# Feed-forward of a hybrid two-block network: first-half weight remainders of the second block's up slabs move from VectorE to GpSimd, and VectorE steps are reordered in attention and at stage borders

## The chip, the cores and the metric

One core of one Trainium2 chip. The metric is the device time of one execution in microseconds (us), smaller is better. Everything is float32 data of 256 tokens by 1024 channels, kept in SBUF from beginning to end, while the weights stream in from HBM.

## The reference

Two blocks of two layers each. The first block: a convolution mixer (layer 0), a recurrence with dilated attention (layer 1), each followed by a feed-forward `(silu(conv(h @ w_gate)) * (h @ w_up)) @ w_down` of width 2816. The second block (layers 2 and 3 here): `x = x + hybrid_mixer(rms_norm(x))`, then

```python
def conv_glu_ffn_2(h, w_up, conv_w, conv_b, w_down):
    u = causal_dwconv_2(h @ w_up, conv_w, conv_b)      # 3 taps, both halves
    gate, val = u[..., :FFN_DIM], u[..., FFN_DIM:]
    return (jax.nn.silu(gate) * val) @ w_down
```

## The kernel before, in words

**Slabs.** All weights are cut into slabs of 128 x 2 x 1024 float32 (two halves of 512 KB). The slabs of all stages form one numbered stream. Each half of a slab passes through four hands: SyncE loads it into `w_raw` (L604), ScalarE rounds it to a high part `w_hi` (L1520, `weights_hi`), VectorE or GpSimd subtracts to get the remainder `w_lo` (`split_lo`, L565), and TensorE multiplies. There are three slots (`WSLOTS = 3`); ScalarE works three slabs ahead (`ROUND_AHEAD`), the remainders two (`SPLIT_AHEAD`). A remainder of half 0 or 1 increments `w_lo[0]` or `w_lo[1]`, always in the order of the slabs; where another engine continues that count, it waits for the one before it (`take_over`, L571). The same count frees `w_raw` for the load of the slab three further on.

**Operands** are also split in two, a rounded and a rest part; `lo_part` (L574) makes a rest.

**The feed-forward** has 22 up slabs, `upA` (14) and `upB` (8), and 12 down slabs, `dnA` (4, between `upA` and `upB`) and `dnB` (8). Layers 2 and 3 are `NORMED_UP`: from up slab 2 on, TensorE works by `paired_halves` (L812 on): eight products of 512 columns with the high part of half 0 (L817), one of half 1, then `slab.wait_split(pe, 0)`, the eight remainder products of 256 columns of half 0 (L821), then `wait_split(pe, 1)`, those of half 1, and the last seven high products.

**Around each up slab c.** ScalarE (`up`, L1590 on) waits until TensorE is done with c, copies two sums out of PSUM (L1595) and increments `up_rest`, rounds a half of slab c + 3, makes the first tap of c (L1604), rounds the hidden value of c - 1 (L1585), rounds the other half, and computes silu (L1617). VectorE (`up`, L2174 on) waits for `up_rest`, adds the two sums (L2182), makes the half 0 remainder of slab c + 2, then the older taps (L2164), the half 1 remainder, and the product of gate and value (L2215), which increments `ffn_prod`. VectorE does this for all up slabs of all four layers, but in layers 2 and 3 the remainders of up slabs 2 and 3 (both halves) are GpSimd's (L697 to 704). GpSimd's loop `up` (L705 on), for slab n, is otherwise only the rest part of the hidden value:

```python
hi, lo = ffn_parts(layer, n)
if n + 2 < count:
    pool.wait_ge(s.up_rest, UP_BEFORE[layer] + off + n + 3 - UP_FIRST[layer])
pool.wait_ge(s.hid_hi, base + off + n + 1)
lo_part(pool, lo, prod[:, j % 2:j % 2 + 1, :], hi).then_inc(s.hid_split, 1)
```

`up_rest` stands at `UP_BEFORE + c + 1 - UP_FIRST` once ScalarE has copied slab c, so this line waits for slab n + 2.

**Elsewhere.** In the dilated attention of layer 1 VectorE masks (`at_mask`, L2373), ScalarE takes exp (`at_exp`), VectorE normalises (`at_probs`), TensorE transposes; the eight units share two `score` buffers. `residual` of ScalarE and GpSimd and `add_residual` of VectorE (L2121) close a stage: the sum into x, the squares for the next norm (`fold_squares`), the rest parts of the next operand (`norm_lo`). In the mixers of layers 2 and 3, `by_token` transposes and the `gates` slabs' remainders of half 1 (VectorE) lie among the state-space steps.

Of the kernel before, what the change touches and what calls it, by code (L numbers as in the profile page):

```python
# [14 lines left out]
P = 128  # L15
# [180 lines left out]
def build(nc, dram):  # L196
    ctx = ExitStack()
    with ctx:  # L198
# [213 lines left out]
        eps = sb("eps", [P, 1])  # L412
        acc = sb("acc", [P, 2, 2, T])
        sil = std[:, :, T:2 * T]
        score = arena[:, 57 * T:65 * T].rearrange("p (b n) -> p b n", b=2)
        cum_parts = sb("cum_parts", [P, T], BF16)
        cum_mid = sb("cum_mid", [SH, T], BF16)
        ident_b = sb("ident_b", [P, SH], BF16)
# [215 lines left out]
        def _(pool):  # L634
# [55 lines left out]
            def ffn(f, n, l=None):  # L690

                sfx, base = stage_ffn(f, l)
                layer = n // 2 - 1

                if layer in NORMED_UP:
                    take_over(pool, "upA" + sfx, 1, l)
                    for k in range(2):  # L697
                        for half in range(2):
                            if k == 1 and half == 1:
                                pool.wait_ge(s.ffn2_tap, 4 * l * FC + 4)  # L700
                            split_lo(pool, slab_at("upA" + sfx, k, l).ahead(SPLIT_AHEAD), half)
                        if k == 0:
                            scaled_lo(UP_OPENING[layer], raw_set(layer))

                def up(off, count):  # L705
                    def body(slab, n, j):
                        hi, lo = ffn_parts(layer, n)
                        if n + 2 < count:
                            pool.wait_ge(s.up_rest, UP_BEFORE[layer] + off + n + 3 - UP_FIRST[layer])
                        pool.wait_ge(s.hid_hi, base + off + n + 1)  # L710
                        lo_part(pool, lo, prod[:, j % 2:j % 2 + 1, :], hi).then_inc(s.hid_split, 1)
                    return body
                slabs("upA" + sfx, up(0, UP_A), l)
                slabs("upB" + sfx, up(UP_A, FC - UP_A), l)
                take_over(pool, "dnB" + sfx, 0, l)
                residual("dnB" + sfx, n, l)

            nc.gpsimd.memset(zeros, 0.0)
# [8 lines left out]

            norm_lo(0, range(DC // 2))
            add_squares(0, 1)
            add_squares(0, 2)  # L730
            pool.wait_ge(s.w_lo[0], 1)
            split_lo(pool, Slab(s, 1), 0)
            opening("ev_cf", 0)
            for stage in ("ev_sc", "ev_b"):
# [58 lines left out]
        def _(pe):  # L793
# [429 lines left out]
            def at_transposes(u):  # L1223
                t = u % 2
                pe.wait_ge(s.at_p, u + 1)
                if u == 0:
                    pe.wait_ge(s.qk_std, COUNT["od_qk"])
                else:
                    pe.wait_ge(s.at_pt, u)
                for b in range(DIL_G * (t + 1)):  # L1230
                    where = tr[:, b * P:b * P + P] if b < 4 else stat[:, T + (b - 4) * P:T + (b - 3) * P]
                    mm = nc.tensor.transpose(where, score[:, u % 2, b * P:b * P + P], ident)
                mm.then_inc(s.at_tr, 1)

            def at_values(p):
# [54 lines left out]
            def layer(l):  # L1290
# [86 lines left out]
                for u in range(4):  # L1377
                    t, kv = u // 2, u % 2
                    if u < 3:
                        pe.wait_ge(s.da_masked, 4 * l + u + 1)  # L1380
                        da_logits(u + 1)
                    pe.wait_ge(s.da_p, 4 * l + u + 1)
                    if u == 0:
                        pe.wait_ge(s.dt_tok, l + 1)
                    else:
                        pe.wait_ge(s.da_out, 4 * l + u)
                    for st in range(t + 1):
                        if st == 1:
                            pe.wait_ge(s.xt_copied, 8 * l + 2 * u)
                        for i in range(QPK):  # L1390
                            mm = nc.tensor.transpose((tr, stat)[st][:, i * P:i * P + P],
                                                     da_score[u % 2][:, i, st * P:st * P + P], ident)
                    mm.then_inc(s.da_tr, 1)
                    slab_products(slab_at("z", 2 * u, l), operand)
                    pe.wait_ge(s.da_pt, 6 * l + (1, 2, 4, 6)[u])
                    for st in range(t + 1):
                        mm = nc.tensor.matmul(tr[:, :], v2[:, st, kv * P:kv * P + P], pt[:, st, 0:4 * P],
                                              start=(st == 0), stop=(st == t))
                    mm.then_inc(s.da_pv, 1)
                    by_token(2 * u)  # L1400
                    if u == 3:
                        pe.wait_ge(s.a_exp, l + 1)
                        pe.wait_ge(s.cum_lo, l + 1)
                        running_sums(0)
                        running_sums(1)
                    if u == 1:
                        slab_products(slab_at("z", 2 * u + 1, l), operand, between=lambda: by_token(3))
                    else:
                        slab_products(slab_at("z", 2 * u + 1, l), operand)
                        by_token(2 * u + 1)  # L1410
# [100 lines left out]
        def _(act):  # L1511
# [36 lines left out]
            def residual(stage, n, gain=None, l=None):  # L1548
# [3 lines left out]
                for k in range(COUNT[stage]):  # L1552
# [12 lines left out]
                            square(j)  # L1565
                    if j == 2 and gain is None:
                        done(slab)
                    if j == 2:
                        root_table()
                if gain is None:  # L1570
                    norm_root(n)
# [241 lines left out]
            def at_exp(u):  # L1813
                n = DIL_G * (u % 2 + 1) * P
                act.wait_ge(s.at_masked, u + 1)
                nc.scalar.activation(score[:, u % 2, 0:n], score[:, u % 2, 0:n], ACT.Exp, scale=-1.0,
                                     bias=small[:, 16 + u:17 + u], accum_out=small[:, 24 + u:25 + u]).then_inc(s.at_exp, 1)

            def at_copy(u):
# [217 lines left out]
        def _(dve):  # L2037
# [80 lines left out]
            def add_residual(stage, l=None, n=None):  # L2118
# [5 lines left out]
                def body(slab, k, j):  # L2124
                    if k < COUNT[stage] - late:
                        weights(slab, halves)
                    if n is not None and k > COUNT[stage] - 4:
                        fold_squares(n, j - 1)
                    slab.wait_done(dve)

# [14 lines left out]
                    if n is not None and j >= 2 and k >= COUNT[stage] - 2:  # L2145
                        if j == 2:
                            weights(slab)
                        norm_lo(n, (2 * j, 2 * j + 1))
                        if j == 3:
                            fold_squares(n, 3)  # L2150
                            weights(slab)
                slabs(stage, body, l)
# [17 lines left out]
            def ffn(f, n, l=None, beside_dn=None):  # L2170
# [3 lines left out]
                def up(off):  # L2174
                    def body(slab, n, j):
# [14 lines left out]
                            tt(zz[:, j, :, :], lin[slab.bank][:, :, :], std[:, 0, 0:T].unsqueeze(1).to_broadcast([P, 2, T]),  # L2190
                               ALU.mult).then_inc(s.bank_free[slab.bank], 1)
                        if c == 2 and layer in NORMED_UP:
                            for half in range(2):
                                dve.wait_ge(s.w_lo[half], slab.number + SPLIT_AHEAD)
                        if opened or layer not in NORMED_UP:
                            weights(slab, (0,))
                        if l is None:
                            dve.wait_ge(s.ffn_t0, base + c + 1)
# [25 lines left out]
                slabs("upA" + sfx, up(0), l)  # L2224
                if beside_dn is not None:
                    beside_dn[0]()
                add_residual("dnA" + sfx, l)
                if beside_dn is not None:
                    beside_dn[1]()
# [144 lines left out]
            def at_mask(u):  # L2374
# [1 line left out]
                t = u % 2  # L2376
                n = (t + 1) * P
                dve.wait_ge(s.at_logits, u + 1)
                if u >= 2:
                    dve.wait_ge(s.at_tr, u - 1)  # L2380
                sc3 = score[:, u % 2, 0:DIL_G * n].rearrange("p (g k) -> p g k", g=DIL_G)
                nc.vector.tensor_tensor_reduce(
                    sc3, at_logit(t),
                    dil[:, DIL_AT[t]:DIL_AT[t] + DIL_G * n].rearrange("p (g k) -> p g k", g=DIL_G),
# [4 lines left out]
            def at_probs(u):  # L2389
                n = (u % 2 + 1) * P  # L2390
                dve.wait_ge(s.at_exp, u + 1)
                ac.link(nc.vector.reciprocal(small[:, 32 + u:33 + u], small[:, 24 + u:25 + u]))
                ts(score[:, u % 2, 0:DIL_G * n], score[:, u % 2, 0:DIL_G * n], small[:, 32 + u:33 + u], None, ALU.mult)\
                    .then_inc(s.at_p, 1)

            qk_norm(0)
# [19 lines left out]
            at_mask(1)  # L2416
            at_probs(0)
            tt(lru_hs[:, :, :], lru_hs[:, :, :], lru_gate[:, :, :], ALU.mult).then_inc(s.lru_y, 1)
            at_mask(2)
            at_probs(1)  # L2420
            dve.wait_ge(s.lru_y_hi, 1)
            lo_part(nc.vector, raw_set(1)[1][:, 0:NC4, :], lru_hs[:, :, :], raw_set(1)[0][:, 0:NC4, :]).then_inc(s.lru_y_lo, 1)
            at_mask(3)
            for u in range(2, 2 * DIL_H):
                if u < 2 * DIL_H - 2:
                    at_probs(u)
                if u == 2 * DIL_H - 3:
                    at_probs(u + 1)
                if u + 2 < 2 * DIL_H:
                    at_mask(u + 2)  # L2430
            at_probs(2 * DIL_H - 1)
            dve.wait_ge(s.att_hi, 1)
            lo_part(nc.vector, raw_set(1)[1][:, NC4:NC4 + 2, :], acc[:, 0, :, :], raw_set(1)[0][:, NC4:NC4 + 2, :]).then_inc(s.att_lo, 1)
            take_over(dve, "od_out", 1)
# [4 lines left out]
            def layer(l):  # L2439
# [236 lines left out]
                def ssd_pair(m):  # L2676
                    if m % 2 == 0:
                        ssd_group(m // 2)
                    ssd_m(2 * m, 2 * m)
                    ssd_m(2 * m + 1, 2 * m + 1)  # L2680
                ssd_pair(0)
                for m in range(XCH // 2):
                    if m + 1 < XCH // 2:
                        ssd_seg(2 * m + 2)
                        ssd_seg(2 * m + 3)
                    if m != 3:
                        weights(slab_at("gates", m, l))
                    ssd_out(2 * m, 2 * m)
                    ssd_out(2 * m + 1, 2 * m + 1)
                    if m == 3:  # L2690
                        weights(slab_at("gates", m, l))
                    if m + 1 < XCH // 2:
                        ssd_pair(m + 1)
# [287 lines left out]
```

## Time and profile before

| | us |
|---|---|
| median of 3 runs (lowest to highest) | 1682.47 (1680.27 to 1682.65) |
| the profiled execution's own time | 1679.26 |
| its span, first to last instruction | 1677.5 |
| TensorE busy | 1654.3 |
| VectorE busy | 1333.7 |
| ScalarE busy | 1086.0 |
| GpSimd busy | 752.4 |

The span is what the trace covers; the 1.8 us between it and the execution's own time lie around it. A share of busy time near 100% says that hardly any time is to be had from that engine's waits, not that it couldn't be made to wait.

### The profile page before, as it was taken

The page shows a single profiled execution, that of the slowest core. Times are in us where ns is not written, and L with a number is a line of the kernel's source. Part 1 is how long each engine was busy: PE and PEld are TensorE (multiplying, and loading weights), DVE is VectorE, ACT ScalarE, POOL GpSimd, SP SyncE. Part 2 cuts the span into 40 slices and gives each one's busy share as a digit, 9 for nine tenths or more (in the row PEclk, how much of TensorE's full clock was granted, in tenths as well). Part 3 has the DMA queues.
Part 4 walks back from the last instruction along what each step waited for, and adds up shares of the span by engine and source line. Part 5 has one row for each costly group of instructions (what it writes and reads, how often), then busy time and mean ns, then how long its engine had stood idle before and what let it go on. Part 6 is the DMA issues. An engine that isn't in the chain of part 4 may idle for free. (4 is left out here: it accounts for less than half of the span.)

```text
span 1677.5 us, 28519 instructions
## 1 busy us (share of the span) xinstructions
PE 1654.3 (99%) x10944; PEld 1491.6 (89%) x10944; DVE 1333.7 (80%) x2204; ACT 1086.0 (65%) x1828; POOL 752.4 (45%) x448
## 2 busy tenths in 40 slices
PE   9999999999999999999999999999999999999997
PEld 8998889998888899998788988899999878888887
DVE  7968887495887887885896699778886689579795
ACT  7676665676765584767653776657577665378572
POOL 7631105872110367764654521057675465351113
PEclk9999999999999999999999999999999999999999
DMA  8445646542555655453445456555455335546552
GB/s 300 163 156 188 223 156 198 189 126 86 179 190 188 195 177 189 165 175 120 137 160 190 153 175 213 166 186 198 153 172 171 126 126 176 176 145 202 191 181 86
DMA packets 81240, 287.10 MB, mean 171 GB/s; under 512 B 9169, under 2 KB 9681, under 8 KB 80977
## 3 DMA queue, kind: packets, MB, share of 16 engines
q1 hardware_dynamic: 79776, 282.10, 50.7%
q10 hardware_dynamic: 1328, 3.18, 0.5%
q8 instruction: 87, 1.43, 0.3%
q14 instruction: 49, 0.39, 0.1%
HBM read 283.90 MB, written 1.05 MB: 170 GB/s over the span
## 5 line engine op out<-in xcount | busy, mean ns | idle before, releaser
L565 POOL TENSOR_TENSOR w_lo<-w_raw,w_hi 128x1024 fp32r<-128x1024 f32 (+2 forms) x239 | 568.4, 2398 | 364.1 <-ACT w_hi L1520 283.0
L1520 ACT ACTIVATE w_hi<-w_raw 128x1024 fp32r<-128x1024 f32 (+1 forms) x544 | 543.1, 1033 | 253.6 <-PE lin L798 163.0
L565 DVE TENSOR_TENSOR w_lo<-w_raw,w_hi 128x1024 fp32r<-128x1024 f32 (+1 forms) x305 | 444.7, 1462 | 30.7 <-ACT w_hi L1520 29.7
L796 PE MATMUL lin<-hid_pair,w_hi 128*128 128x256 f32 x1152 | 329.9, 286 | 1.7 <-DVE hid_pair L574 1.7
L797 PE MATMUL lin<-hid_pair,w_hi 128*128 128x256 f32 x1152 | 325.9, 283 | 0.0
L798 PE MATMUL lin<-hid_pair,w_lo 128*128 128x256 f32 x1152 | 325.9, 283 | 0.0
L796 PEld LDWEIGHTS lin<-hid_pair,w_hi 128*128 128x128 f32 x1152 | 220.9, 192 | 4.1 <-issue 3.3
L797 PEld LDWEIGHTS lin<-hid_pair,w_hi 128*128 128x128 f32 x1152 | 221.0, 192 | 0.3
L798 PEld LDWEIGHTS lin<-hid_pair,w_lo 128*128 128x128 f32 x1152 | 220.9, 192 | 0.0
L574 POOL TENSOR_TENSOR hid_pair<-arena,hid_pair 128x256 fp32r<-128x256 f32 x64 | 56.5, 887 | 294.4 <-ACT std L1595 175.7
L817 PE MATMUL logit<-h_pair,w_hi 128*128 128x512 f32 x540 | 146.7, 392 | 0.0
L817 PE MATMUL lin<-h_pair,w_hi 128*128 128x512 f32 x540 | 135.0, 390 | 3.2 <-DVE arena L2182 2.8
L2164 DVE SCALAR_TENSOR_TENSOR acc<-arena,par,acc 128x254 f32<-128x254 f32 (+1 forms) x264 | 119.8, 495 | 7.5 <-ACT acc L1604 4.6
L817 PEld LDWEIGHTS lin<-h_pair,w_hi 128*128 128x128 f32 x540 | 101.1, 188 | 25.4 <-DVE arena L2182 3.7
L817 PEld LDWEIGHTS logit<-h_pair,w_hi 128*128 128x128 f32 x540 | 97.2, 189 | 17.4
L796 PE MATMUL lin<-h_pair,w_hi 128*128 128x256 f32 x320 | 92.9, 290 | 0.9 <-DVE h_pair L574 0.8
L797 PE MATMUL lin<-h_pair,w_hi 128*128 128x256 f32 x320 | 90.5, 283 | 0.0
L798 PE MATMUL lin<-h_pair,w_lo 128*128 128x256 f32 x320 | 90.5, 283 | 0.0
L817 PE MATMUL logit<-hid_pair,w_hi 128*128 128x512 f32 x324 | 89.1, 392 | 0.0
L796 PE MATMUL lin<-w_hi,hid_pair 128*128 128x512 f32 (+1 forms) x224 | 87.0, 388 | 0.0
L797 PE MATMUL lin<-w_lo,hid_pair 128*128 128x512 f32 (+1 forms) x224 | 84.0, 375 | 0.0
L798 PE MATMUL lin<-w_hi,hid_pair 128*128 128x512 f32 (+1 forms) x224 | 84.0, 375 | 0.0
(413 smaller groups left out, 3508.2 us busy)
## 6 DMA issues: line engine op xcount, KB each, us to landing
w_raw<-in_upA SPq DMA_DIRECT2D x112, 512.0 KB, 4.4
w_raw<-in_upB SPq DMA_DIRECT2D x64, 512.0 KB, 4.6
w_raw<-in_xbc SPq DMA_DIRECT2D x48, 512.0 KB, 4.3
w_raw<-in_dnA SPq DMA_DIRECT2D x32, 512.0 KB, 4.3
w_raw<-in_dnB SPq DMA_DIRECT2D x32, 512.0 KB, 3.9
w_raw<-in_z SPq DMA_DIRECT2D x32, 512.0 KB, 4.5
w_raw<-in_gates SPq DMA_DIRECT2D x32, 512.0 KB, 4.1
w_raw<-in_ps SPq DMA_DIRECT2D x32, 512.0 KB, 4.0
```

The costliest lines, as they stand in the source:

```text
L565: eng.tensor_tensor(w_lo[slab.slot][:, half, part], w_raw[slab.slot][:, half, part], w_hi[slab.slot][:, half, part].bitcast(F32), ALU.subt ...
L574: return eng.tensor_tensor(lo, whole, hi.bitcast(F32), ALU.subtract)
L796: nc.tensor.matmul(out, lhs[0], rhs[0], start=first, stop=False)
L797: nc.tensor.matmul(out, lhs[0], rhs[1], start=False, stop=False)
L798: return nc.tensor.matmul(out, lhs[1], rhs[0], start=False, stop=last)
L817: return nc.tensor.matmul(outs[half], tile_of(slab, half, k)[0], pairs[k], start=(k == 0), stop=(half == 1 and k == last))
L1520: nc.scalar.activation(w_hi[slab.slot][:, half, part], w_raw[slab.slot][:, half, part], ACT.Copy)\
L2164: ins = stt(outs[i][:, d:T], ins_[i][:, 0:T - d], weight(taps - 1 - d, i), outs[i][:, d:T], ALU.mult, ALU.add)
```

## The change

In the up stages of layers 2 and 3, GpSimd makes the half 0 remainder of slab n + 2 at the head of its body for slab n, from n = 2 of `upA` to the end of `upB`; VectorE makes it no more there, and takes the count over at `dnA`, GpSimd at `upB`. GpSimd's remainder of half 1 of up slab 3 waits for the first product of VectorE, not for its first taps. In the attention there are three `score` buffers, and VectorE's masks and normalisations come in another order. At a stage border `fold_squares(n, 2)` comes behind the last residual sum instead of ahead of it; for `od_out`, `norm_lo` of chunks 4 and 5 and the loading of ScalarE's root table also come later. One `by_token` moves between two halves of a `z` slab, one `gates` remainder behind two other steps, and at the start two lines of GpSimd change places.

```diff
-        score = arena[:, 57 * T:65 * T].rearrange("p (b n) -> p b n", b=2)
+        score = arena[:, 57 * T:66 * T].rearrange("p (b n) -> p b n", b=3)
@@ GpSimd, ffn
                             if k == 1 and half == 1:
-                                pool.wait_ge(s.ffn2_tap, 4 * l * FC + 4)
+                                pool.wait_ge(s.ffn_prod, base + 1)
                             split_lo(pool, slab_at("upA" + sfx, k, l).ahead(SPLIT_AHEAD), half)
@@
                         hi, lo = ffn_parts(layer, n)
+                        if layer in NORMED_UP and off + n >= 2:
+                            split_lo(pool, slab.ahead(SPLIT_AHEAD), 0)
                         if n + 2 < count:
                             pool.wait_ge(s.up_rest, UP_BEFORE[layer] + off + n + 3 - UP_FIRST[layer])
                         pool.wait_ge(s.hid_hi, base + off + n + 1)
@@
                 slabs("upA" + sfx, up(0, UP_A), l)
+                if layer in NORMED_UP:
+                    take_over(pool, "upB" + sfx, 0, l)
                 slabs("upB" + sfx, up(UP_A, FC - UP_A), l)
-                take_over(pool, "dnB" + sfx, 0, l)
+                if layer not in NORMED_UP:
+                    take_over(pool, "dnB" + sfx, 0, l)
@@ GpSimd, start
+            pool.wait_ge(s.w_lo[0], 1)
             add_squares(0, 2)
-            pool.wait_ge(s.w_lo[0], 1)
@@ TensorE, z slabs
-                    if u == 1:
-                        slab_products(slab_at("z", 2 * u + 1, l), operand, between=lambda: by_token(3))
+                    if u in (1, 2):
+                        slab_products(slab_at("z", 2 * u + 1, l), operand, between=lambda: by_token(2 * u + 1))
@@ ScalarE, residual
-                    if j == 2:
+                    if j == (3 if stage == "od_out" else 2):
                         root_table()
@@ VectorE, add_residual
-                    if n is not None and k > COUNT[stage] - 4:
+                    if n is not None and COUNT[stage] - 4 < k < COUNT[stage] - 1:
                         fold_squares(n, j - 1)
                     slab.wait_done(dve)
@@
                         if j == 2:
                             weights(slab)
-                        norm_lo(n, (2 * j, 2 * j + 1))
+                            if stage != "od_out":
+                                norm_lo(n, (4, 5))
                         if j == 3:
+                            if stage == "od_out":
+                                norm_lo(n, (4, 5))
+                            fold_squares(n, 2)
+                            norm_lo(n, (6, 7))
                             fold_squares(n, 3)
@@ VectorE, ffn
                         if c == 2 and layer in NORMED_UP:
-                            for half in range(2):
-                                dve.wait_ge(s.w_lo[half], slab.number + SPLIT_AHEAD)
-                        if opened or layer not in NORMED_UP:
+                            dve.wait_ge(s.w_lo[1], slab.number + SPLIT_AHEAD)
+                        if layer not in NORMED_UP:
                             weights(slab, (0,))
@@
+                if layer in NORMED_UP:
+                    take_over(dve, "dnA" + sfx, 0, l)
                 add_residual("dnA" + sfx, l)
@@ VectorE, attention
-                if u >= 2:
-                    dve.wait_ge(s.at_tr, u - 1)
-                sc3 = score[:, u % 2, 0:DIL_G * n].rearrange("p (g k) -> p g k", g=DIL_G)
+                if u >= 3:
+                    dve.wait_ge(s.at_tr, u - 2)
+                sc3 = score[:, u % 3, 0:DIL_G * n].rearrange("p (g k) -> p g k", g=DIL_G)
@@
-            at_mask(2)
             at_probs(1)
             dve.wait_ge(s.lru_y_hi, 1)
             lo_part(nc.vector, raw_set(1)[1][:, 0:NC4, :], lru_hs[:, :, :], raw_set(1)[0][:, 0:NC4, :]).then_inc(s.lru_y_lo, 1)
+            at_mask(2)
             at_mask(3)
             for u in range(2, 2 * DIL_H):
-                if u < 2 * DIL_H - 2:
-                    at_probs(u)
-                if u == 2 * DIL_H - 3:
-                    at_probs(u + 1)
+                at_probs(u)
                 if u + 2 < 2 * DIL_H:
                     at_mask(u + 2)
-            at_probs(2 * DIL_H - 1)
@@ VectorE, gates
-                    if m != 3:
+                    if m not in LATE_WEIGHTS:          # (3, 5)
                         weights(slab_at("gates", m, l))
                     ssd_out(2 * m, 2 * m)
                     ssd_out(2 * m + 1, 2 * m + 1)
-                    if m == 3:
+                    if m in LATE_WEIGHTS:
                         weights(slab_at("gates", m, l))
```

## Rows read from the trace of the kernel before

**Rows 1.** The page: busy us of the engines (share, instructions); granted TensorE clock, 40 slices.

```profile
PE 1654.3 (99%) x10944; PEld 1491.6 (89%) x10944; DVE 1333.7 (80%) x2204; ACT 1086.0 (65%) x1828; POOL 752.4 (45%) x448
...
PEclk9999999999999999999999999999999999999999
```

**Rows 2.** Waits of TensorE (who waited for whom: us in total, times, longest).

```profile
PE lin L817 <- DVE arena L2182: 2.8, 2, 1.4
...
PE lin L796 <- DVE hid_pair L574: 1.7, 1, 1.7
PE logit L821 <- DVE w_lo L565: 1.3, 2, 0.7
...
PE tr L1421 <- DVE sq L2668: 0.8, 2, 0.4
...
PE lin L796 <- DVE h_pair L574: 0.8, 1, 0.8
PE stat L1391 <- DVE arena L2617: 0.7, 2, 0.3
```

**Rows 3.** Timeline, all engines, one up slab of layer 2 (start, us, what, [idle before]).

```profile
1006.02 1.98 PE L817 MATMUL lin<-h_pair,w_hi 128*128 128x512 f32 x8
1006.22 0.38 ACT L1595 ACTIVATE std<-lin 128x256 f32<-128x256 f32 x1 [1.23 <-PE logit L817]
...
1006.76 1.06 ACT L1520 ACTIVATE w_hi<-w_raw 128x1024 fp32r<-128x1024 f32 x1
1006.91 0.42 DVE L2182 TENSOR_TENSOR arena<-lin,std 128x256 f32<-128x256 f32 x1 [0.51 <-ACT std L1595]
1006.95 0.74 POOL L574 TENSOR_TENSOR hid_pair<-arena,hid_pair 128x256 fp32r<-128x256 f32 x1 [4.83 <-ACT std L1595]
...
1007.58 1.22 DVE L565 TENSOR_TENSOR w_lo<-w_raw,w_hi 128x1024 fp32r<-128x1024 f32 x1
...
1007.83 1.13 PEld L821 LDWEIGHTS lin<-h_pair,w_lo 128*128 128x128 f32 x8
...
1008.83 1.67 DVE L2164 SCALAR_TENSOR_TENSOR acc<-arena,par,acc 128x255 f32<-128x255 f32 x4
...
1010.41 1.22 DVE L565 TENSOR_TENSOR w_lo<-w_raw,w_hi 128x1024 fp32r<-128x1024 f32 x1
...
1011.58 1.98 PE L817 MATMUL lin<-h_pair,w_hi 128*128 128x512 f32 x8
```

**Rows 4.** Waits over all engines: GpSimd's hidden-rest subtraction behind ScalarE's copy, layers 2, 3.

```profile
POOL hid_pair L574 <- ACT std L1595: 175.7, 28, 30.6
...
POOL hid_far L574 <- ACT std L1595: 38.6, 8, 4.8
```

**Rows 5.** Groups by form, GpSimd: weight remainder (busy, mean ns, idle before and releasers).

```profile
L565 POOL TENSOR_TENSOR w_lo<-w_raw,w_hi 128x1024 fp32r<-128x1024 f32 x213 | 519.4, 2459 | 293.9 <-ACT w_hi L1520 220.2 <-PE logit L1374 32.3 <-DVE w_lo L565 13.2
```

**Rows 6.** Timeline, opening of the up stage of layer 2 (the same 532 us later in layer 3).

```profile
964.00 2.39 POOL L565 TENSOR_TENSOR w_lo<-w_raw,w_hi 128x1024 fp32r<-128x1024 f32 x1 [2.56 <-DVE acc L2164]
964.01 2.66 DVE L2215 TENSOR_TENSOR arena<-std,acc 128x256 f32<-128x256 f32 x1
964.42 1.98 PE L817 MATMUL lin<-h_pair,w_hi 128*128 128x512 f32 x8
...
971.54 2.14 PE L817 MATMUL lin<-h_pair,w_hi 128*128 128x512 f32 x8 [1.40 <-DVE arena L2182]
...
974.29 0.37 ACT L1595 ACTIVATE std<-lin 128x256 f32<-128x256 f32 x1
...
978.18 1.98 PE L817 MATMUL lin<-h_pair,w_hi 128*128 128x512 f32 x8
```

**Rows 7.** Timeline, attention of layer 1: VectorE's remainder behind GpSimd's.

```profile
380.72 1.82 POOL L565 TENSOR_TENSOR w_lo<-w_raw,w_hi 128x768 fp32r<-128x768 f32 x1 [4.12 <-ACT w_hi L1520]
380.76 2.85 DVE L574 TENSOR_TENSOR hid_pair<-arena,hid_pair 128x1024 fp32r<-128x1024 f32 x1
```

**Rows 8.** DMA of layer 2's feed-forward: halves of up slabs (count, KB, median us to landing).

```profile
w_raw<-in_upA SPq DMA_DIRECT2D x16, 512.0 KB, 4.5
```

More of the change, by code:

```diff
@@ L1231, in at_transposes @@
                     where = tr[:, b * P:b * P + P] if b < 4 else stat[:, T + (b - 4) * P:T + (b - 3) * P]
-                    mm = nc.tensor.transpose(where, score[:, u % 2, b * P:b * P + P], ident)
+                    mm = nc.tensor.transpose(where, score[:, u % 3, b * P:b * P + P], ident)
                 mm.then_inc(s.at_tr, 1)
@@ L1815, in at_exp @@
                 act.wait_ge(s.at_masked, u + 1)
-                nc.scalar.activation(score[:, u % 2, 0:n], score[:, u % 2, 0:n], ACT.Exp, scale=-1.0,
+                nc.scalar.activation(score[:, u % 3, 0:n], score[:, u % 3, 0:n], ACT.Exp, scale=-1.0,
                                      bias=small[:, 16 + u:17 + u], accum_out=small[:, 24 + u:25 + u]).then_inc(s.at_exp, 1)
@@ L2392, in at_probs @@
                 ac.link(nc.vector.reciprocal(small[:, 32 + u:33 + u], small[:, 24 + u:25 + u]))
-                ts(score[:, u % 2, 0:DIL_G * n], score[:, u % 2, 0:DIL_G * n], small[:, 32 + u:33 + u], None, ALU.mult)\
+                ts(score[:, u % 3, 0:DIL_G * n], score[:, u % 3, 0:DIL_G * n], small[:, 32 + u:33 + u], None, ALU.mult)\
                     .then_inc(s.at_p, 1)
@@ L2680, in ssd_pair @@
                     ssd_m(2 * m + 1, 2 * m + 1)
+                LATE_WEIGHTS = (3, 5)
                 ssd_pair(0)
```

## The prediction

> **What bounds the kernel now.** The page comes first: TensorE is busy for 1654.3 of 1677.5 us, at the upper clock level (2.4 GHz) in all 40 slices [rows 1]. So at most 23 us could be won from its waits, and 80% of VectorE or 45% of GpSimd says nothing by itself: work moved between them pays only where TensorE waits for it, and costs wherever it comes to wait. The second view is the waits of TensorE [rows 2]. Those that touch the change are small: 2.8 us in two waits for VectorE's sum in the up stages of layers 2 and 3, 1.3 us in two for a weight remainder there, 1.7 and 0.8 us in layer 1, 0.7 and 0.8 us in the mixers. The third view is the timeline of one up slab in layer 2 [rows 3], to be read as a list of deadlines. TensorE starts it at 1006.02 and the next at 1011.58, a period of 5.57 us. It needs the half 0 remainder at 1007.83 (the weight load of L821), 1.81 us after the start. VectorE has it ready long before, as it makes it two slabs ahead. VectorE's own list (two sums of 0.42, two remainders of 1.22, four taps of 1.67, a product of 0.42) is 5.4 of the 5.57 us: full, but in time, since from one slab to the next TensorE starts without a wait.
>
> **The main part: half 0 on GpSimd.** What counts is not GpSimd's load but its order. In its body for slab n the new remainder (for slab n + 2) stands first, and behind it the old wait for `up_rest` of slab n + 2. That wait really is the last to end there: GpSimd's rest of the hidden value starts right behind ScalarE's copy 28 + 8 = 36 times [rows 4], which is 12 + 6 in each of two layers, all bodies with n + 2 < count. Queued behind the wait is now the head of the next body: the remainder for slab n + 3. But `up_rest` of n + 2 comes when TensorE is done with n + 2, that is, when it has started n + 3, whose remainder has not been begun. Two slabs of lead become none.
>
> The price per slab, from TensorE's start of the slab at 1006.02 [rows 3]: ScalarE copies twice from 1006.22, GpSimd's rest subtraction starts at 1006.95 and lasts 0.74, so it is free at 1007.69, 1.67 after the start. A remainder of 1024 columns takes 2459 ns in the mean on GpSimd [rows 5], mostly about 2.40 (2.39 in [rows 6]). I take 2.40, since in the stretch concerned VectorE has nothing to run until its taps: ready at 4.07, and with 0.1 us for the two semaphore steps at 4.17. It is needed at 1.81, so TensorE waits 2.36 us, in every such slab, as each slab's copy comes from TensorE's own end: a loop that cannot catch up. Nothing covers it; TensorE has no other work between L817 and L821.
>
> The count: in `upA` the remainder stands behind a wait in bodies 2 to 12 (slabs 4 to 13 and `dnA` 0: 11), in `upB` in bodies 1 to 6 (slabs 3 to 7 and `dnB` 0: 6). Body 0 of `upB` has no wait ahead of it; body 13 of `upA` and body 7 of `upB` wait only for `hid_hi`, and their targets are a whole slab later. That is 17 per layer, of which slab 4 is apart.
>
> The opening [rows 6]. Before, GpSimd's half 1 of slab 3 starts at 964.00, at the same time as VectorE's first product, which then takes 2.66 us in place of 0.42 and ends with it. The changed wait makes the product go first, so VectorE gains 2.2 us and GpSimd loses 0.45. The half is then ready at about 966.9, and TensorE needs it about 2.8 us after its start of slab 3 at 964.42, so at 967.2: just in time. ScalarE's copies for slab 2 come about 1.4 earlier, VectorE's sum with them, and the wait of 1.40 ahead of slab 4 (971.54) goes: it can start at 964.42 + 5.57 = 970.0. But its remainder hangs on the copies for slab 3, which ScalarE, behind TensorE here, makes at 974.29 and would make at some 973.1 to 973.7. Plus 0.66 + 0.74 + 2.40 + 0.1 the remainder is there at 976.9; needed at 971.8 to 972.0. Slab 4 ends at about 970.0 + 5.57 + 4.9 = 980.5, where before slab 5 starts at 978.18: 2.3 us later, with the gained 1.4 and the old remainder wait of 0.66 [rows 2] already in it.
>
> Sum per layer: 2.3 + 16 x 2.36 = 40.1 us; two layers 80 us. What VectorE saves (17 times 1.22 and more) is worth nothing beyond the opening, since it was not waited for. Its taps may be blocked until GpSimd is done: from 4.07 they, the half 1 remainder and the product take 1.67 + 1.22 + 0.42, till 7.4, within the new period of 7.93. The load of half 0 is issued when the remainder is done, 4.1 after the start; landing takes 4.5 us [rows 8], so 8.6, and ScalarE wants it at 7.93 + 0.74 = 8.67 [rows 3]. Tight, but ScalarE's copies stand ahead of it. The take-over at `dnA` holds VectorE until about 7.2 us after the start of `dnA` 0; its next sums are due behind that slab anyway: nothing.
>
> In [rows 6] a VectorE operation with both inputs in SBUF ends only with the GpSimd one it met. The Trainium skill, page "SBUF — State Buffer", section "Who interferes with whom", calls this an exclusive lock of a shared port pair held for the whole instruction; by that rule alone the move would exchange 1.22 us of VectorE for up to 2.40 us of blocking, a loss where VectorE has 0.2 us to spare, while by the rows the stall of TensorE comes first and gives VectorE its time back.
>
> **The other parts.** Attention: TensorE waits 1.69 us for VectorE's rest part, which takes 2.85 us in place of about 1.2, beside GpSimd's remainder at 380.72 [rows 2, 7]. Ahead of it stood a mask that itself waited for logits; with that mask behind it, it starts at about 379.1 and is done before 380.72: -1.7. The plain order of the later units could move some tenths either way; I take 0. Border of `od_out`: the residual sum comes earlier, two rest parts later, the wait of 0.8 us [rows 2] falls to about 0.3: -0.5. At the other borders TensorE did not wait and its next operand parts are not put off: 0. The `z` transposes (two waits, 0.7) and the `gates` remainder at m = 5 (two waits, 0.8): both go at best, -1.5; at worst none does. At the start, the first remainder is done ahead of the last squares, so the exchanged wait is met already: 0. Together -3.7 us, bounds 0 and -6.
>
> **Sum** against the profiled execution: 1679.26 + 80.2 - 3.7 = 1755.8 us. It ran 3.2 us below the median; on the median the same difference of 76.5 gives 1759.0.
>
> **Bounds of the main term.** Least: with the mean lead of the copies 0.1 shorter, no semaphore time, the remainder at 2.39: 2.2 per slab, 75 in all. A GpSimd operation that yields to a started VectorE operation could add 0.4 per slab: 2.76, 94 in all. With the bounds of the rest: +69 to +94.
>
> **Rivals.**
> First, no lateness (faster). If the count in `up_rest` meant a slab earlier, the remainder would be ready one period before: 4.07 - 5.57 = 1.5 us ahead of the start, with 3.3 to spare. It decides at GpSimd's chain of 4.17 us against the 1.81 of TensorE. Then only the small waits are won: 2.8 + 1.3 + 3.7 = 7.8, so 1674.7. Against it stand the 36 releases by ScalarE's copy of the slab that has just ended [rows 3, 4]. Chance 0.04.
> Second, the loop gets longer through ScalarE: the late load (8.6 against 8.67) and blocked taps push silu past the end of the slab, and the copies with it. At 0.5 to 1 us in each of 34 slabs, +17 to +34: 1776 to 1793. For it speaks that both margins are under 0.6 us; against, that the copies come ahead of the rounding that needs the load. Chance 0.07.
> Third, TensorE's clock. Every slice was granted 2.4 GHz [rows 1], with waits of at most 1.7 us past the start [rows 2]; the new ones are 2.4 and 4.9 us. If it fell to 1.2 GHz in these 34 slabs, each would take 11.1 us, and the remainder would be nearly in time, so +3.2 us a slab over the forecast: +108, 1867. The Trainium skill, page "TensorE: Matmul & The Clock Gate", section "What's actually happening", lets the clock fall after idleness; by that the two waits of 4.9 us are the likeliest place. If only there, it costs a few us, inside the range. Chance of the full case 0.03.
> The forecast keeps 0.86.
>
> **Range and chances.** The main case spans 1751 to 1776; for its unseen ends (a shorter chain, a brief clock fall, some of the second rival) I take 1746 to 1778. About 0.2% (3.4 us) is what a measurement of this kernel tells from no change. Slower 0.95, same 0.01, faster 0.04.
>
> **What would show it.** Right: in the changed trace TensorE waits over 2 us at L821 for GpSimd's L565 in 34 places, a period of about 7.9 us in the up stages, a first such wait of about 5 us; the wait at 971.54 and the long product at 964.01 gone; total waits of TensorE up by about 77 us; the wait of 1.7 us in attention gone. Wrong: GpSimd's remainder starting before ScalarE's copies of the slab ahead, a period of 5.57 kept, or a granted clock below 1.

## The result, and the profile after

The changed kernel takes 1771.93 us (median of 4 runs, 1770.28 to 1772.96) against 1682.22 before: ratio 1.0535, 95% interval 1.0516 to 1.0553. It is 89.7 us slower; 76.5 were forecast, and the time lies inside the range. The profiled execution has a span of 1768.5 us, 91.0 more than before.

The page of the changed kernel, its first and second part:

```profile
span 1768.5 us, 28515 instructions
PE 1685.1 (95%) x10944; PEld 1508.9 (85%) x10944; DVE 1312.5 (74%) x2164; ACT 1084.3 (61%) x1828; POOL 845.9 (48%) x488
...
PE   9999999999999999999998779899999999977978
...
PEclk9999999999999999999999889999999999989999
```

40 remainders have moved (DVE x2204 to x2164, POOL x448 to x488). TensorE's busy time has grown by 30.8 us though it does the same 10944 products: part of them ran at the lower clock, in the slices where its busy share is down too. These are the up stages of layers 2 and 3.

The waits of TensorE (who waited for whom: us in total, times, longest), the longest four:

```profile
PE lin L826 <- POOL w_lo L565: 68.8, 34, 4.9
PE logit L1087 <- POOL arena L731: 2.1, 1, 2.1
PE lin L1104 <- DVE h_pair L574: 1.0, 1, 1.0
PE stat L1132 <- ACT arena L1739: 0.7, 1, 0.7
```

L826 is L821 of the kernel before. 34 waits for GpSimd's weight remainder, one of 4.9 us in each layer, the others of 1.85. Of [rows 2] the 2.8, the 1.3 and the 1.7 are gone.

One up slab of layer 2 in the timeline (start, us, what, idle before); it answers to [rows 3]:

```profile
1003.09 1.98 PE L822 MATMUL lin<-h_pair,w_hi 128*128 128x512 f32 x8
1003.29 0.38 ACT L1600 ACTIVATE std<-lin 128x256 f32<-128x256 f32 x1 [3.89 <-PE logit L822]
...
1004.02 0.75 POOL L574 TENSOR_TENSOR hid_pair<-arena,hid_pair 128x256 fp32r<-128x256 f32 x1 [6.14 <-ACT std L1600]
...
1004.73 2.36 POOL L565 TENSOR_TENSOR w_lo<-w_raw,w_hi 128x1024 fp32r<-128x1024 f32 x1
...
1005.90 2.65 DVE L2174 SCALAR_TENSOR_TENSOR acc<-arena,par,acc 128x255 f32<-128x255 f32 x4 [1.16 <-ACT acc L1609]
...
1007.14 1.00 PEld L826 LDWEIGHTS lin<-h_pair,w_lo 128*128 128x128 f32 x8 [2.27 <-POOL w_lo L565]
...
1010.76 1.98 PE L822 MATMUL lin<-h_pair,w_hi 128*128 128x512 f32 x8
```

The loop is there as described: TensorE's end, ScalarE's copies, GpSimd's rest part, GpSimd's remainder, TensorE again. The load of the remainder comes 4.05 us after the start of the slab (1007.14 - 1003.09), where before it came at 1.81, and the period is 7.67 us in place of 5.57: 2.10 more. VectorE's taps take 2.65 us in place of 1.67, as they hardly advance until GpSimd's remainder ends (1004.73 + 2.36 = 1007.09).

Not every slab is that short. The differences between the starts of the slabs in layer 2, read from the timeline of TensorE, are these periods from up slab 2 on (each of them 5.57 before, except 6.02, 7.12 and 6.64 for slabs 2, 3 and 4); `dnA` 1 to `upB` 2, which don't wait, are left out:

```
slab   2     3     4      5    6     7     8     9     10    11    12    13    dnA0
us     5.84  5.59  12.32  9.20 7.67  9.21  7.67  9.23  7.67  9.22  7.67  7.67  9.20
upB    3     4     5     6     7     dnB0
us     7.67  7.67  9.20  7.67  9.21  7.67
```

Layer 3 has seven long ones too (and 12.59 for slab 4): 14 slabs of 9.2. What they are is seen in the stretches (us, busy and instructions of the engines, PEclk, DMA share, GB/s) of one of them and of a short one:

```profile
996.00:1000.00 4.00, 2.15 (x15) 2.07 (x15) 3.31 (x5) 2.33 (x5) 1.88 (x1) 0.88 0.27 65
1000.00:1004.00 4.00, 4.00 (x16) 3.33 (x16) 0.84 (x3) 0.71 (x3) 0.00 (x0) 0.69 0.53 202
...
1008.00:1012.00 4.00, 4.00 (x24) 3.51 (x24) 2.37 (x6) 1.46 (x4) 0.30 (x1) 1.00 0.80 262
```

After the wait that ends at 997.93 the granted clock is below full until about 1003 (16 products in 4 us); after the one that ends at 1007.14 it is 1.00 (24 products in 4 us). Between 1000 and 1004 it was at its lower level, 1.2 GHz, for part of the time.

The 91 us between the two profiled spans, by stages (the clock's part in slab 4 is in its row):

| | us |
|---|---|
| 32 slabs, 2.10 each | +67.2 |
| 14 of them, 1.54 each for the clock | +21.6 |
| slab 4, two layers (12.32, 12.59 against 6.64) | +11.6 |
| slabs 2 and 3, two layers (5.84 + 5.59 against 6.02 + 7.12) | -3.4 |
| start -1.2, attention and the border of `od_out` -2.9, mixers of layers 2 and 3 -1.0 each | -6.1 |

### The profile page after: what moved, and what is told of

Same layout as the page of the kernel before. It is cut to its first block and busy times, and to the rows that moved or that the text cites. A ratio compares the mean times of both kernels' runs of the same rounds, so it can differ in the third digit from the quotient of the medians.

```text
span 1768.5 us, 28515 instructions
## 1 busy us (share of the span) xinstructions
PE 1685.1 (95%) x10944; PEld 1508.9 (85%) x10944; DVE 1312.5 (74%) x2164; ACT 1084.3 (61%) x1828; POOL 845.9 (48%) x488
## 5 line engine op out<-in xcount | busy, mean ns | idle before, releaser
L565 POOL TENSOR_TENSOR w_lo<-w_raw,w_hi 128x1024 fp32r<-128x1024 f32 (+1 forms) x279 | 664.9, 2397 | 385.8 <-ACT w_hi L1525 306.4
L565 DVE TENSOR_TENSOR w_lo<-w_raw,w_hi 128x1024 fp32r<-128x1024 f32 (+1 forms) x265 | 392.8, 1487 | 37.9 <-ACT w_hi L1525 36.9
L2174 DVE SCALAR_TENSOR_TENSOR acc<-arena,par,acc 128x254 f32<-128x254 f32 (+1 forms) x264 | 162.4, 654 | 52.9 <-ACT acc L1609 51.4
L822 PE MATMUL logit<-h_pair,w_hi 128*128 128x512 f32 x540 | 157.6, 416 | 0.0
L826 PE MATMUL lin<-h_pair,w_lo 128*128 128x256 f32 x540 | 81.1, 293 | 61.5 <-POOL w_lo L565 61.5
L826 PEld LDWEIGHTS lin<-h_pair,w_lo 128*128 128x128 f32 x540 | 73.1, 194 | 77.0 <-POOL w_lo L565 74.1
L822 PEld LDWEIGHTS logit<-h_pair,w_hi 128*128 128x128 f32 x540 | 106.5, 207 | 20.0
L803 PE MATMUL lin<-h_pair,w_lo 128*128 128x256 f32 x320 | 90.5, 283 | 0.0
L801 PE MATMUL lin<-w_hi,hid_pair 128*128 128x512 f32 (+1 forms) x224 | 87.0, 388 | 0.0
```

What stands on the lines that cost most here:

```text
L565: eng.tensor_tensor(w_lo[slab.slot][:, half, part], w_raw[slab.slot][:, half, part], w_hi[slab.slot][:, half, part].bitcast(F32), ALU.subt ...
L801: nc.tensor.matmul(out, lhs[0], rhs[0], start=first, stop=False)
L803: return nc.tensor.matmul(out, lhs[1], rhs[0], start=False, stop=last)
L822: return nc.tensor.matmul(outs[half], tile_of(slab, half, k)[0], pairs[k], start=(k == 0), stop=(half == 1 and k == last))
L826: return nc.tensor.matmul(outs[half][:, 0, :], tile_of(slab, half, k)[1], pairs[k][:, 0, :], start=False, stop=(half == 0 and k == last))
L2174: ins = stt(outs[i][:, d:T], ins_[i][:, 0:T - d], weight(taps - 1 - d, i), outs[i][:, d:T], ALU.mult, ALU.add)
```

## The experiments

**Half 0 back on VectorE.** All else stays as changed.

```diff
-                        if layer in NORMED_UP and off + n >= 2:
-                            split_lo(pool, slab.ahead(SPLIT_AHEAD), 0)
...
-                        if layer not in NORMED_UP:
+                        if opened or layer not in NORMED_UP:
                             weights(slab, (0,))
```

(with the hand-overs at `upB`, `dnA` and `dnB` as before)

> The changed kernel with one part undone: VectorE makes the half 0 remainders of the up slabs of layers 2 and 3 again, everything else stays as changed. Theory (the remainder queued behind the wait for the slab just ended is the whole loss): the 34 waits of 4.9 and 1.85 us are gone, the period of an up slab is 5.57 us again, TensorE's clock is 1.00 throughout, and the small gains stay: about 1674 us, 8 below the kernel before. Rival (some of the loss comes from the reordered borders, attention or gates): it stays above 1682.

1669.33 us, ratio 0.9941 to the kernel before (0.9926 to 0.9956), granted clock 0.999. The period is 5.57 us again and no wait for GpSimd's remainder is left in the up stages. So the move of half 0 costs 102.6 us (1771.93 - 1669.33), and all the rest of the change gains, by more than forecast. This version is faster than both kernels, by 0.6% than the one before.

**Without the wait for `up_rest`.** GpSimd keeps half 0.

```diff
-                        if n + 2 < count:
+                        if n + 2 < count and layer not in NORMED_UP:
                             pool.wait_ge(s.up_rest, ...)
```

> The changed kernel, GpSimd's half 0 remainders kept, but its rest subtraction no longer waits for up_rest of slab n + 2 in layers 2 and 3 (only for the rounded hidden value of n, which ScalarE makes one slab earlier). Order theory: the remainder for slab n + 3 is ready some 6.5 us after the start of slab n + 2, a slab ahead of its use, so TensorE does not wait for it: within 1674 to 1682. Rival (GpSimd's remainder of 2.4 us in place of VectorE's 1.2 us, and the blocking between the two engines, is what costs): VectorE's taps are blocked behind it, its work for a slab grows to over 5.57 us, and 0.3 to 0.6 us a slab are lost, 1685 to 1700.

1748.68 us, ratio 1.0413 (1.0396 to 1.0431): neither case came true. The period is 7.58 us. The timeline of a slab:

```profile
1003.48 4.27 DVE L2174 SCALAR_TENSOR_TENSOR acc<-arena,par,acc 128x255 f32<-128x255 f32 x4 [1.16 <-ACT acc L1609]
...
1003.84 0.74 POOL L574 TENSOR_TENSOR hid_pair<-arena,hid_pair 128x256 fp32r<-128x256 f32 x1 [4.33 <-ACT hid_pair L1590]
1004.04 1.98 PE L822 MATMUL lin<-h_pair,w_hi 128*128 128x512 f32 x8
1004.53 2.55 POOL L565 TENSOR_TENSOR w_lo<-w_raw,w_hi 128x1024 fp32r<-128x1024 f32 x1
...
1007.68 1.21 DVE L565 TENSOR_TENSOR w_lo<-w_raw,w_hi 128x1024 fp32r<-128x1024 f32 x1
```

Without the wait GpSimd's two operations start, one behind the other, as soon as ScalarE has rounded the hidden value, which is when VectorE starts its taps. The taps then take 4.27 us in place of 1.67, everything of VectorE and ScalarE for the slab comes later, and with it the rounding that GpSimd waits for: another loop, now through the blocked taps. TensorE waits at both halves (31.8 us in 33 waits for GpSimd, 19.8 us in 35 for VectorE). The old wait put most of GpSimd's work where VectorE reads PSUM or has nothing to do. The rival had the mechanism, but put it at 0.3 to 0.6 us a slab, and it costs 2.0 (7.58 - 5.57).

**Three slabs ahead.** The same place in GpSimd's queue, behind the same wait, but the remainder is that of slab n + 3.

```diff
-                        if layer in NORMED_UP and off + n >= 2:
-                            split_lo(pool, slab.ahead(SPLIT_AHEAD), 0)
+                        if layer in NORMED_UP and off and n == 0:
+                            split_lo(pool, slab.ahead(SPLIT_AHEAD), 0)
+                        if layer in NORMED_UP and 1 - off // UP_A <= n < count - 1:
+                            split_lo(pool, slab.ahead(SPLIT_AHEAD + 1), 0)
```

> The changed kernel, with GpSimd's half 0 remainder made three slabs ahead in place of two in the up stages of layers 2 and 3, at the same place in its queue, behind the same wait. Order theory: it is begun at the same moment of each slab but one slab earlier than it is needed; no wait of TensorE for it. GpSimd's and VectorE's operations meet exactly as in the changed kernel, so the taps take 2.65 us in place of 1.67. If VectorE's list then ends before the slab does, about 1675; if the blocked taps make VectorE the bound, its list is 0.9 + 1.0 + 1.1 + 2.65 + 1.2 + 0.4, about 6 us a slab against 5.57, and 34 x 0.4 = 14 us are lost, 1689. Speed theory (GpSimd is too slow whatever the order): still over 1740.

1684.64 us, ratio 1.003 (1.0019 to 1.0041). One slab of lead gives back 87 of the 103 us: the loss was the order, not GpSimd's speed. The period in `upA` is 5.90 us, and its timeline shows why not 5.57:

```profile
1011.66 2.41 POOL L565 TENSOR_TENSOR w_lo<-w_raw,w_hi 128x1024 fp32r<-128x1024 f32 x1
1011.80 1.09 ACT L1611 ACTIVATE acc<-arena,par 128x256 f32<-128x256 f32 x2 [0.62 <-DVE arena L2194]
...
1012.93 2.60 DVE L2176 SCALAR_TENSOR_TENSOR acc<-arena,par,acc 128x255 f32<-128x255 f32 x4 [1.16 <-ACT acc L1611]
...
1015.45 1.22 DVE L565 TENSOR_TENSOR w_lo<-w_raw,w_hi 128x1024 fp32r<-128x1024 f32 x1
```

The taps last 0.9 us longer than unblocked ones, and VectorE's chain, with ScalarE's first taps in it, is the bound of `upA`: sums, first taps, the older taps, the half 1 remainder, the product, 5.90 us in a circle. All of `upB` is back at 5.57; slab 4 (7.65) and `dnA` 1 (7.78) are longer, and so is `dnB` 1 (6.22). The 1.22 us that GpSimd takes off VectorE in each slab do not make up for the blocked taps, since they are not saved: in the kernel before, that remainder fills the time in which ScalarE makes the first taps [rows 3]; here VectorE is idle there for 1.16 us (the bracket behind the taps). The loss against the version with half 0 on VectorE is 15.3 us, where the second case of the expectation had 14; its six terms add up to 7.25 us and not to about 6, so the closeness is in part luck.

**TensorE kept busy in its wait.** In the changed kernel, products of zeros ahead of `wait_split(pe, 0)`; nothing is left out, they write to a bank that isn't read.

```diff
                 both_parts(1, 0)
+                for _ in range(fill):
+                    nc.tensor.matmul(tr[:, 0:T], zeros[:, 0:P], zeros, start=True, stop=True)
                 slab.wait_split(pe, 0)
```

First with twelve:

> The changed kernel with 12 products of zeros of 256 columns put on TensorE ahead of its wait for the half 0 remainder, in the slabs of the up stages of layers 2 and 3 that wait (not in the two down slabs that do). They lie in time in which it would be idle. If the clock's fall in the changed kernel (14 slabs of 9.2 us in place of 7.67, and the first one of each layer) comes of TensorE being idle in each slab, the clock stays at 2.4 GHz, each period is 7.67 us, and the time is 14 x 1.54 = 22 us shorter or somewhat more: about 1748. If the longer slabs have another cause, such as the load of the weights or ScalarE, nothing changes: 1772.

1835.13 us in one run. The twelve took 5.18 us a slab (10.75 - 5.57), more than the wait, so the forecast of 1748 failed and the time says nothing. It does say something of the clock: its mean is 0.997, and the 15 filled slabs of layer 2 all take 10.75 or 10.76 us (slab 4 10.91), none 1.5 more. Then with four:

> As the filled kernel, but with 4 products of zeros in place of 12. The 12 took 0.43 us each, 5.18 us a slab (a period of 10.75 = 5.57 + 5.18), more than the wait; 4 take 1.73 us, within the 1.85 us that TensorE waits. If idleness is what lets the clock fall, the clock stays at 2.4 GHz and the period at 7.67 in every filled slab: 12 of the 14 slabs of 9.2 us lose their 1.54, the first of each layer some 1 to 2 us less: 1772 - 18 - 3 = about 1750. If something else makes those slabs long: 1772.

1751.66 us in one run, the mean clock 0.996 in place of 0.982. In layer 2 the filled slabs after slab 4 all take 7.68 to 7.71 us. Long are only slab 4 (12.18; it still waits 3.2) and `dnB` 0 (9.21), which isn't filled. So TensorE's idleness in each slab is what let the clock fall, and it cost about 20 us (1771.93 - 1751.66, the latter from a single run); slab 4 and `dnB` 0, which still wait, are also where the clock still fell. It also shows that the 7.67 are the loop's: with the clock up the period stays there, filled or not.

**The start and the first product alone**, in the kernel before.

```diff
-            add_squares(0, 2)
             pool.wait_ge(s.w_lo[0], 1)
+            add_squares(0, 2)
...
-                                pool.wait_ge(s.ffn2_tap, 4 * l * FC + 4)
+                                pool.wait_ge(s.ffn_prod, base + 1)
```

> The kernel before with two parts of the change alone: the two lines changed at GpSimd's start, and its half 1 remainder of up slab 3 waiting for the first product. If the lock between the two engines is what both act on: at the start, TensorE's wait of 1.1 us for a remainder blocked by GpSimd goes (1.2 us), and at each opening VectorE's first product takes 0.42 in place of 2.66 us and the wait of 1.4 us goes (1.4 to 1.7 each): -4.0 to -4.6 us. If the gain of 1.2 at the start in the changed kernel came of data that landed earlier: -3.0.

1678.53 us, ratio 0.9977 (0.9967 to 0.9987), by the medians 3.3 us less. The opening does as forecast: VectorE's first product takes 0.43 us in place of 2.66, slab 3 takes 5.56 us in place of 7.12, slab 4 6.48 in place of 6.64, so 1.7 us a layer. The start doesn't belong to the change: TensorE reaches its first norm at 15.97 us here, at 17.76 before, and at 16.23 and 16.28 in the next two kernels, which don't have the swapped lines. The swap is worth 0.3 us at most, not the 1.2 of the first case of the expectation; the openings alone, 3.4 us, make the whole difference of the medians.

**Attention alone**, in the kernel before: the three `score` buffers and the new order.

> The kernel before with the attention part alone: three score buffers, masks and normalisations in the new order. The wait of 1.7 us for VectorE's rest part, which GpSimd's remainder blocks, goes, as it starts 2.9 us earlier: -1.7 to -2.5 us. If only the order at the end of attention mattered: 0 to -0.5.

1675.74 us (8 runs, 1675.26 to 1676.78), ratio 0.9972 (0.9961 to 0.9982): 6.0 us less, where the trace, from the first logits to the first product of the next feed-forward's second slab, is only 2.2 us shorter than in the profile of before (50.46 against 52.68). The other 4 us are in executions of another kind than the profiled one of the kernel before. The kernel of the last experiment (start and first product) has the old attention, and its profiled execution is of that kind. The stretch from 380 to 395 us (columns as above), in the kernel before and in that one:

```profile
380.00:395.00 15.00, 13.30 (x103) 10.32 (x102) 9.53 (x23) 8.34 (x19) 1.82 (x1) 1.00 0.11 37
```

```profile
380.00:395.00 15.00, 13.31 (x68) 10.21 (x69) 6.53 (x14) 5.89 (x14) 1.15 (x1) 0.66 0.11 36
```

After the same wait of 1.7 us the clock fell to its lower level, and the attention took 57.25 us in place of 52.68. The runs of the kernel before in that comparison spread from 1677.19 to 1683.52 (27 runs), those of the new attention alone over 1.5 us (8 runs). The mean granted clock of each run splits the 27: six, at 1677.19 to 1678.68, had 0.998 or 0.999, and 21, at 1680.30 to 1683.52, had 0.994 to 0.997. All eight of the new attention had 0.998 or 0.999. So the clock fell in most executions of the kernel before; that it fell in attention is seen only in two profiles of kernels with the same attention, this one and the next, and inferred for the others.

**The border alone**, in the kernel before: `fold_squares`, `norm_lo` and `root_table` as changed.

> The kernel before with the border part alone: the fold of squares behind the last residual sum, the later root table and rest parts at od_out. Forecast in the prediction: -0.5 us, at od_out alone. The changed kernel was about 1.8 us further ahead of the one before behind attention than at its start, border included; if the border is worth more than forecast, -1 to -2.

1679.61 us, ratio 0.9987 (0.9976 to 0.9998). Its attention had the fall of the clock too; against the kernel with the start and the first product, which had it as well, the same stretch is 0.9 us shorter (56.37 against 57.25), and the wait of 0.8 us [rows 2] is gone. The medians differ by 2.2 us, but four of its ten runs had a clock of 0.998 or more against 6 of the 27, so that is not the border's worth alone.

**One remainder more on GpSimd**, in the best version, for its last two waits (0.66 us each, at slab 4).

```diff
                             scaled_lo(UP_OPENING[layer], raw_set(layer))
+                    split_lo(pool, slab_at("upA" + sfx, 2, l).ahead(SPLIT_AHEAD), 0)
```

> The version with VectorE's half 0 remainders and all other parts of the change, plus one remainder more on GpSimd: half 0 of up slab 4 in layers 2 and 3, right behind half 1 of slab 3, so before the opening's waits. It takes 1.22 us off VectorE where TensorE waits for it (two waits of 0.66 us at slab 4). If the remainder is made between VectorE's taps of slab 1 at no cost to them: -1.3 us, 1668. If it blocks those taps for its 2.4 us, the sum of slab 2 comes 1.5 to 2.4 us later and TensorE waits for it again: +2 to +4, about 1672.

1674.0 us, ratio 0.9966 (0.9949 to 0.9982), so 4.7 us worse than the version that it was made from:

```profile
959.09 4.94 POOL L565 TENSOR_TENSOR w_lo<-w_raw,w_hi 128x1024 fp32r<-128x1024 f32 x2 [3.46 <-DVE arena L2220]
```

```profile
960.77 4.32 DVE L2170 SCALAR_TENSOR_TENSOR acc<-arena,par,acc 128x255 f32<-128x255 f32 x4 [1.16 <-ACT acc L1605]
```

Between two GpSimd operations that follow each other little gets through; the taps of slab 1 last 4.32 us in place of 1.67, and TensorE waits 2.0 us in each layer for the sum of slab 2, as the second alternative said. In layer 3 the clock fell right behind that wait (eight products of 512 columns took 3.42 us in place of 2.12); in layer 2 it did not.

## Why the prediction was right, point by point

**The main step held.** The order, the loop, the count (34 waits, 17 a layer) and the position of each were as worked out from the code and [rows 3, 4]. The list of TensorE's waits grew by 60 us (14.7 to 75.1), where some 77 were expected. But one of the prediction's own signs of being wrong came true as well: a granted clock below 1. Undone alone, the kernel is fast; with one slab more of lead, nearly so. The rival of no lateness fell with the 34 waits.

**Mis-sized: the wait per slab**, 2.36 us in the sum, 2.10 measured. GpSimd's remainder took 2.36 where 2.40 was taken, it started 1.64 after the slab's start and not 1.67, and the hand-over to TensorE took 0.05 us where 0.1 was taken; that moves the load from 4.17 to 4.05. The load comes 2.24 later than in the kernel before, the period grows by 2.10; the 0.14 between them lie in how loads and products overlap, which no run here takes apart. The wait that the profile shows is 1.85. 32 times 0.26 is 8 us too much.

**Mis-sized, and the largest error: the clock.** The third rival had it fall for whole slabs, at 108 us and a chance of 0.03, and otherwise for a few us at the two long waits. It fell in between: in 14 slabs for a part of the slab, 21.6 us, and in slab 4, where in layer 2 the stretch from the first remainder product to the last seven high products took 3.43 us (971.96 to 975.39) against 2.01 in a short slab, so 1.4 us, and in layer 3 some 1.7. Together 25 us. The range held it because it was drawn wide for such things, and by luck: the two errors point opposite ways. Had the wait cost the 2.36 us of the sum, with the clock as it was, the time would have been about 1780, above the upper bound of 1778. The page "TensorE: Matmul & The Clock Gate" of the Trainium skill, section "What's actually happening", lets the clock fall after idleness; the trace agrees, and shows that repeated waits of 1.85 us are enough, where the prediction had looked at the two of 4.9 alone.

**The opening** was right but for that: 5.84 + 5.59 for slabs 2 and 3, and the wait at slab 4 was 4.91 us where 4.9 stood in the sum. That closeness is in part luck: ScalarE's copies came 2.8 us after the start of slab 4 where 3.1 was taken, and GpSimd's rest part, which met a VectorE operation, took 1.38 us where 0.74 was taken. VectorE's first product takes 0.43 us where 0.42 stood.

**VectorE and the load** were no bound in the changed kernel, as forecast: the second rival's loop through blocked taps did not close, and ScalarE's rounding starts 0.74 us after the start of the slab, as before (1003.83 - 1003.09), so the load was not late. But it is real: without GpSimd's wait, it costs 7.58 us a slab, and with three slabs ahead 5.90. The exclusive hold of the port, as the Trainium skill's page "SBUF — State Buffer" has it in the section "Who interferes with whom", agrees with all of it: taps of 1.67 us last 2.65, 4.27 or 4.32, according to what GpSimd does, and GpSimd's rest part of 0.74 lasts 1.38 where VectorE was first. It is not a full stop from the first tap to GpSimd's end: of the 1.67 us, some 0.2, 0.3 and 0.6 were done in the three cases while GpSimd ran, by what was left when it ended.

**The other parts**, -3.7 forecast, are -6.1 in the profile. Attention and border gave 2.9 (2.2 forecast), the mixers 2.0 (1.5), and 1.2 at the start belong to the execution. In the medians they are worth more: the version with all of them and without the moved remainder is 11 us below the kernel before. Its profile is 10.3 us shorter, 1.9 of it at the start, so 8.4 are by the waits, 3.4 of these the openings; the 2.6 left fit the clock in attention, which costs 4.6 us in part of the executions only. The step that failed there is that the wait of 1.7 us in attention was priced as 1.7 us.

## What to carry to other kernels

When work is put into another engine's queue, ask first what stands ahead of it and whose end that waits for; a remainder that was made two slabs ahead had no lead at all once it stood behind one waiting line. Then ask what the engine that is relieved will do with its time: if it only waits for the next hand, nothing is saved. Then ask what the other engine blocks while it runs: GpSimd's operations with SBUF operands are best placed where VectorE reads PSUM or waits. And price a repeated short wait of TensorE at more than its length.

## What the runs showed of the hardware

- Waits of TensorE of 1.85 us, once in 7.67 us, lowered its clock in about every second slab; with 1.73 us of products of zeros in each, it stayed up.
- Behind one wait of 1.7 us in the attention it fell in some executions (0.66 granted over 15 us) and not in others (1.00), at a cost of about 4.6 us: a part of what seemed scatter of the kernel before. Behind a wait of 2.0 us it fell in layer 3 and not in layer 2 of one execution.
- A VectorE operation with two SBUF inputs hardly advances while a GpSimd subtraction of SBUF data runs (four taps of 1.67 us lasted 2.65), and between two of GpSimd's that follow each other VectorE gets little in: the taps lasted 4.32 beside two remainders. Sums with one input in PSUM (0.42) were not slowed.
- A product of zeros of 256 float32 columns takes 0.43 us (5.18 us for 12).
